# A decoder step's SwiGLU stage: second-pass token sums moved from VectorE to GpSimd, token splits moved behind the combinations, and the first W_down pieces requested ahead of the block loads

## The reference, cut to what matters

```python
hf = rms_norm(x, g_ffn_pre)
f = (jax.nn.silu(hf @ w_gate) * (hf @ w_up)) @ w_down
x = x + rms_norm(f, g_ffn_post)
```

## Time and profile before

| | before |
|---|---|
| median of three runs | 2591.41 us |
| profiled execution: its time | 2599.37 us |
| profiled execution: its span | 2597.6 us |
| mean granted TensorE clock | 0.978 |
| TensorE busy | 2454.0 us, 94% |
| VectorE busy | 1574.9 us, 61% |
| ScalarE busy | 1138.5 us, 44% |
| GpSimd busy | 321.6 us, 12% |

### The profile page before, as it was taken

How to read it: one execution, slowest core, us unless ns; L and a number is a source line. 1 busy time by engine, 2 the same in 40 slices (tenths; PEclk the granted TensorE clock), 3 DMA queues, 4 the chain that set the end, 5 groups by cost and what they waited for, 6 DMA issues and landing times. The chain is left out here.

```text
span 2597.6 us, 45864 instructions
## 1 busy us (share of the span) xinstructions
PE 2454.0 (94%) x16716; PEld 1411.0 (54%) x16924; DVE 1574.9 (61%) x3679; ACT 1138.5 (44%) x2680; POOL 321.6 (12%) x696
## 2 busy tenths in 40 slices
PE   7999987899999999999888999999999989999997
PEld 4557765476858677645444444444444434444453
DVE  6658876676766666778676655555655763122322
ACT  5559985454545454443454433343343443111211
POOL 1002220011202111211100022212200000000202
PEclk9999998999999999999899999999999999999999
DMA  6431345601011111344222344444432454344645
GB/s 224 136 98 54 105 128 167 201 18 43 26 51 50 35 34 61 110 154 148 89 86 72 92 138 128 133 130 142 138 90 69 114 164 146 136 162 146 182 154 98
DMA packets 274919, 289.15 MB, mean 111 GB/s; under 512 B 15549, under 2 KB 235720, under 8 KB 273280
## 3 DMA queue, kind: packets, MB, share of 16 engines
q1 hardware_dynamic: 264426, 251.52, 31.4%
q0 software_dynamic: 10272, 34.70, 5.1%
HBM read 191.20 MB, written 94.97 MB: 110 GB/s over the span
## 5 line engine op out<-in xcount | busy, mean ns | idle before, releaser
L118 PE MATMUL m_ps_then_y<-w_in_then_w_out_lo,act 128*128 128x256 bf16 x640 | 174.4, 273 | 0.1
L119 PE MATMUL m_ps_then_y<-w_in_then_w_out_lo,act 128*128 128x256 bf16 x640 | 174.4, 273 | 0.0
L120 PE MATMUL m_ps_then_y<-w_in_then_w_out_lo,act 128*128 128x256 bf16 x640 | 174.4, 273 | 0.0
L2948 PE MATMUL f_bank<-act,f_sums_and_w_then_down 128*128 128x512 bf16 x382 | 145.6, 381 | 8.5 <-ACT f_hidden_then_hidden L3083 7.7
L2949 PE MATMUL f_bank<-act,f_sums_and_w_then_down 128*128 128x512 bf16 x395 | 150.5, 381 | 0.9
L2947 PE MATMUL f_bank<-act,f_sums_and_w_then_down 128*128 128x512 bf16 x384 | 146.3, 381 | 0.9 <-DVE f_mid L3333 0.6
L2069 DVE SCALAR_TENSOR_TENSOR y_then_w_out<-z_then_patterns,m_hd,y_then_w_out 128x512 f32<-128x512 f32 x120 | 90.2, 752 | 89.2 <-ACT y_then_w_out L1803 86.4
L119 PE MATMUL m_ps_then_y<-act,w_in_then_w_out_lo 128*128 128x512 bf16 (+1 forms) x400 | 133.0, 351 | 6.7 <-DVE w_in_then_w_out_lo L2036 4.9
L120 PE MATMUL m_ps_then_y<-act,w_in_then_w_out_lo 128*128 128x512 bf16 (+1 forms) x394 | 130.0, 350 | 0.0
L118 PE MATMUL m_ps_then_y<-act,w_in_then_w_out_lo 128*128 128x512 bf16 (+1 forms) x382 | 125.5, 348 | 1.0 <-ACT z_then_patterns L1800 0.7
L2948 PE MATMUL f_bank<-mix_m_lo_then_tokens,f_sums_and_w_then_down 128*128 128x512 bf16 x320 | 121.3, 379 | 0.9
(11 more groups left out here) (697 smaller groups left out, 7053.0 us busy)
## 6 DMA issues: line engine op xcount, KB each, us to landing
hidden_blocks<-f_h_block SPq DMA_DIRECT2D x66, 256.0 KB, 2.7
m_w_raw<-in_w_gate SPq DMA_DIRECT2D x30, 512.0 KB, 3.8
m_w_raw<-in_w_up SPq DMA_DIRECT2D x30, 512.0 KB, 4.0
f_t_then_hidden<-hidden_blocks SPq DMA_DIRECT2D x18, 704.0 KB, 5.5
f_hidden_then_hidden<-hidden_blocks SPq DMA_DIRECT2D x18, 704.0 KB, 5.5
hidden_blocks<-mix_m_hi_then_tokens SPq DMA_DIRECT2D x44, 256.0 KB, 2.6
hidden_blocks<-mix_m_lo_then_tokens SPq DMA_DIRECT2D x44, 256.0 KB, 2.9
act<-in_w_down POOLq DMA_DIRECT2D x22, 512.0 KB, 5.9
```

The source lines that it names most:

```text
L118: pe.matmul(out, w_hi, x_hi, start=first, stop=False, skip_group_check=in_parts)
L119: pe.matmul(out, w_hi, x_lo, start=False, stop=False, skip_group_check=in_parts)
L120: return pe.matmul(out, w_lo, x_hi, start=False, stop=last, skip_group_check=in_parts)
L2948: nc.tensor.matmul(bank[:, :], high, t_lo[q][j][:, kt, :], start=False, stop=False, skip_group_check=True)
```

## The change

1. The four token sums of the second pass (`t_sum_up`) go to the head of GpSimd's stream, in the order T1, T3, T2, T4, with waits: T1 for the split of the sample difference, the others as before.
2. `T_IN_UNIT` replaces `T_STEPS`: one token split a unit, in units 1 to 7, in the order B11, T1, T3, B21, T2, T4, B22. On VectorE it stands behind `combine_away` instead of ahead of `combine_near`. On ScalarE its place within the unit stays.
3. SP requests the pieces of W_down one unit earlier (units 39 to 42), behind that unit's weight loads, and the block loads 0 and 1 in units 42 and 43, behind the pieces. The units in which the pieces are split stay the same.

```diff
-T_STEPS = {1: [(0, B11), (1, T1)], 2: [(0, T1), (1, T3)], 3: [(0, T3), (0, B21)], 4: [(1, T2), (0, T2)], 5: [(1, T4), (0, T4)], 6: [(0, B22)]}
-T_IN_UNIT = {n: [j for summed, j in steps if not summed] for n, steps in T_STEPS.items()}
+T_IN_UNIT = {n: [j] for n, j in enumerate(T_ORDER[1], 1)}
...
+        def tail_pieces(n):
+            first = (n - UNITS + TAIL) * TAIL_PIECES
+            return min(first, D_PAIRS), min(first + TAIL_PIECES, D_PAIRS)
...
-                    if n == UNITS - TAIL:
-                        load_hidden(0)
-                        load_hidden(1)
-                    if n >= UNITS - TAIL:
-                        for i in range((n - UNITS + TAIL) * TAIL_PIECES, min((n - UNITS + TAIL + 1) * TAIL_PIECES, D_PAIRS)):
+                    if n >= UNITS - TAIL - 1:
+                        for i in range(*tail_pieces(n + 1)):
                             load_down(i)
+                    if n >= UNITS - 2:
+                        load_hidden(n - UNITS + 2)
...
@@ gpsimd @@
+                def t_sum_up(j):
+                    x11, x12 = quarter(g.x32, 1, False, False), quarter(g.x32, 1, False, True)
+                    x21, x22 = quarter(g.x32, 1, True, False), quarter(g.x32, 1, True, True)
+                    if j == T1:
+                        pool.wait_ge(t_low, t_at(0, X_SD))
+                        one, other, how = x12, x11, ALU.subtract
+                    elif j == T3:
+                        pool.wait_ge(t_sums, sum_at(1, T1))
+                        one, other, how = x22, x12, ALU.subtract
+                    elif j == T2:
+                        pool.wait_ge(t_sums, sum_at(1, T3))
+                        pool.wait_ge(t_low, t_at(1, B11))
+                        one, other, how = x12, x11, ALU.add
+                    else:
+                        pool.wait_ge(t_sums, sum_at(1, T2))
+                        pool.wait_ge(t_low, t_at(1, B21))
+                        one, other, how = x21, x11, ALU.subtract
+                    nc.gpsimd.tensor_tensor(t_from(1, j), one, other, how).then_inc(t_sums, 1)
...
+                for j in SUM_ORDER[1]:
+                    t_sum_up(j)
                 for i in range(D_PAIRS):
...
@@ vector, unit(n) @@
-                    for step in T_STEPS.get(n, ()):
-                        if step[0]:
-                            t_sum_up(step[1])
-                        else:
-                            t_split(1, step[1])
                     combine_near(n)
...
                     combine_away(n)
+                    for j in T_IN_UNIT.get(n, ()):
+                        t_split(1, j)
                     if fresh:
                         w_split(k + 1, S4)
```

More of the change, by code:

```diff
@@ L3121, in unit @@
                     if n >= UNITS - TAIL:
-                        for i in range((n - UNITS + TAIL) * TAIL_PIECES, min((n - UNITS + TAIL + 1) * TAIL_PIECES, D_PAIRS)):
+                        for i in range(*tail_pieces(n)):
                             down_high(i)
@@ L3258, in sample_difference @@
                                             ALU.subtract).then_inc(t_sums, 1)
[L3260 to L3271, removed]
-                    else:
-                        dve.wait_ge(t_sums, sum_at(1, T2))
-                        dve.wait_ge(t_low, t_at(1, B21))
-                        one, other, how = x21, x11, ALU.subtract
-                    nc.vector.tensor_tensor(t_from(1, j), one, other, how).then_inc(t_sums, 1)
                 def keep_low(n, b):
```

## The result

The changed kernel takes 2565.82 us (median of four runs, 2561.58 to 2567.37) against 2592.76 for the kernel before: ratio 0.9892, 95% interval 0.9867 to 0.9917, so about 27 us faster. The forecast was 2563.

The account below looks back on a forecast made before the run. TensorE, busy 94% of the span, was taken as the bound, with time to gain only at its waits and low clock. 31.5 + 9.8 - 12.9 = 28.4 us brings the median from 2591.4 to 2563; range 2549 to 2578.

Parts of the forecast that it names:

- What is in reach: TensorE's waits for f_mid and ScalarE's line 3083, with the low-clock matmuls behind them: 41.3 us the change can reach.
- Sums and splits leave the place ahead of `combine_near`: Units 1 to 6: moving both VectorE steps closes the gaps ahead of A22 and their low-clock stretches, 31.5 us.
- A sum on GpSimd takes 4.5 us: Each 2048-column token sum on GpSimd, estimated from rows of 512 columns and one column: 4.5 us, at most 5.1.
- Unit 0: T1 and T3 on GpSimd hold VectorE, so ScalarE's bank copy and TensorE's S3 come late: price 7.7 us.
- Unit 2: T2 runs across the unit's start and holds VectorE, so S2 and A22 come late: price 3.6 us.
- Unit 5: T4 runs across the unit's start and makes S2 late by 1.6 us, no more, since the unit has slack.
- Together 12.9, or 7.9 in the other order: Price of GpSimd's sums in units 0, 2 and 5: 12.9 us, or 7.9 if VectorE's back-to-back operations keep GpSimd out.
- The pieces: W_down pieces requested a unit earlier, ahead of the block loads, end TensorE's wait behind unit 40's late pieces: 9.8 us.
- (a): Rival: GpSimd's hold on VectorE hardly costs; gain 36 to 41 us, time 2550 to 2555; chance 0.14.
- (b): Rival: the earlier W_down pieces don't help, as the tail waits for something else; gain 18.6 us, 2573; chance 0.07.
- (c): Rival: even units have no slack, so the moved split pushes TensorE; gain 17 us, about 2577; chance 0.15.
- (d): Rival: a GpSimd sum over four strided rows far dearer than 4.5 us; 2601 at 14 us a sum; chance 0.06.

Follow-up runs that it names:

- the version without any wait: The changed kernel with the four sums on VectorE where it has room (unit 1, ends of units 2, 4 and 6): 2550.79 us, ratio to before 0.9833.
- sums by rows: The changed kernel with each GpSimd sum cut into four operations of one row (512 columns): 2558.50 us, ratio to before 0.9857.

## Why the prediction was right, point by point

- **What is in reach** (41.3 us): all of it went. What came back are new waits. For the token steps the version without any wait gives the size: 193.6 less 161.5, 32.1 us, for the 31.5 forecast. The matmuls at 1.2 GHz cost 9.2 us and not 9.6, since the first and the last of a stretch run only partly at that level, and the six waits weigh 1.0 more than their brackets.
- **Sums and splits leave the place ahead of `combine_near`** (21.95 us of waits and 9.6 at the low clock): right. Units 1, 3, 4 and 6 have no wait. The moved split at no cost, with 0.1 us of room in units 2 and 4: right, unit 4 shows none, and in the version without GpSimd's sums all units run at 19.53 us. "Some 2 us to spare" in odd units: right, a sum of 2.2 us stood there in units 1 and 5 without a wait.
- **A sum on GpSimd takes 4.5 us**: 4.53 where VectorE wasn't ahead, 4.83 to 4.84 in the other three.
- **Unit 0, 7.7 us**: 7.4 (a wait of 4.68 and the matmuls at 1.2 GHz), by the steps that were worked out: T1 ahead of the S3 split, one VectorE operation between T1 and T3, then the bank copy.
- **Unit 2, 3.6 us**: 3.1 by the distance of the units (its waits are 2.5). The step that was too dear is "sixteen VectorE operations and the waits between them": late as VectorE was, ScalarE had caught up, and VectorE's waits for it, 0.42 and 1.29 us (the second is in rows 5), were gone. **Unit 5, 1.6 us**: 1.4, and no more.
- **Together 12.9, or 7.9 in the other order**: 11.9 in the three units, 12.3 against the version without sums on GpSimd. The order was the first one. T2 was asked for while a VectorE split ran and took 0.3 us longer for it, between two GpSimd operations VectorE got one turn, and VectorE's back-to-back operations don't keep GpSimd out. The Trainium skill (SBUF — State Buffer, "Who interferes with whom") says that issue order decides who is held. The trace agrees for the operation that is running; the 7.9 came from taking it for a whole run of VectorE's operations, and here the two engines took turns.
- **The pieces, 9.8 us**: 9.64. The first block had 15 us for the 16 forecast.
- **The sum**, 28.4 us: 29.4 in the stage, since the price was 0.6 too dear and the reach 0.6 too small. The profiled execution fell by 32.0, the median by 27; the 2.6 us by which the first is over 29.4 lie outside the stage, and the nearness of the median to 2563 owes something to luck, as four executions of the kernel before lie up to 11 us apart.
- **Rivals.** (a) a small price of the lock: false, it was 12.3 us, and 5.9 even with operations of one row. (b) false: 9.64 us came off behind unit 8. (c) false: no wait in units 4 and 6. (d) false: the sum over four rows takes the 4.5 us that were worked out from 512 columns and one.

## What to carry to other kernels

An idle engine is not free if its operations hold those of the busy one. Here a GpSimd sum held VectorE's operations with two SBUF inputs for its whole length, so moving 2.3 us of work over could cost up to 4.8 us of the engine it was meant to relieve. The same work at a place with room on VectorE was worth 12 us more. If it must go to GpSimd, cut it short: one row at a time made 6.5 us of difference. Starting it where VectorE reads PSUM would be the next thing to try; no run here did. And look first at where a step stands: with the sums left on VectorE, moving the splits from between a finished product and the one that waited for it gave 26.2 us, more than the whole change to the token steps.

## What the runs showed of the hardware

- The hold goes both ways: GpSimd's sum took 4.53 us when it started on its own and 4.83 with a VectorE two-input operation in flight; rows of 1.28 us took 1.6 to 1.7 beside VectorE's weight sums, and the one asked for during the split of B22 (3.35 us) took 3.31.
- Under such load they alternate, one operation each (sums by rows, 1298 to 1311 us).
- GpSimd's fills of 1.8 us hold nothing. The Trainium skill (SBUF — State Buffer, "Who interferes with whom") says so of a GpSimd operation that only writes.
- A VectorE operation with one input from PSUM isn't held: in the kernel with sums by rows one took 0.68 us at 1340.92, inside a GpSimd row that ran from 1340.41 to 1342.14.
- A wait of TensorE of about 2 us is followed by matmuls at the 1.2 GHz level in some places and not in others: after the two waits of 1.95 and 1.96 us in the kernel with sums on VectorE at their old places, 8 matmuls at 0.43 us and none.
- The start of the stage in the profiled executions ranges from 1283.4 to 1294.3 us, with nothing changed ahead of it. The waits between that start and the second half repeat within 0.1 us, the low-clock stretches within 1.5. So spans differ by more than most of the effects, and stretches of the timeline between two marks tell them apart. Most of those 11 us arise between 555 and 1080 us: the first matmul into `m_ps_h` starts at 550 to 555 us in all of them, the first into `o_ps_y` at 1076.7 to 1087.6. The mean granted clock from 555 to 1076 us was 0.98 in the four that came last there (1086.3 us and later) and 0.99 or 1.00 in the others.
